# The skip term of a chunked scan as diagonal matrix products on TensorE, with one GpSimd sum left

## What is computed

```
y_fwd = ssd_chunked(xs, dt[:, :, 0], a_neg[0], bm, cm)
y_bwd = flip(ssd_chunked(flip(xs), flip(dt[:, :, 1]), a_neg[1], flip(bm), flip(cm)))
y = y_fwd + y_bwd + d_skip.astype(jnp.float32).reshape(SSD_GROUPS, hg)[..., None] * xs
y = y.reshape(b, s, SSD_INNER) * jax.nn.silu(z.astype(jnp.float32))
```

## Time and profile before

| | us |
|---|---|
| runs | 2482.91, 2483.04, 2487.15; median 2483.04 |
| profiled execution, its own time | 2485.22 |
| span of its trace | 2483.4 |
| PE busy in the span | 2426.9 (98%) |
| chain that ended last: PE 81%, DVE 9%, ACT 4%, POOL 3%, issue 2%, DMA 1% | |
| chunk loop, layer 0, start of L1081 of chunk 0 to low part of chunk 0 after the loop | 404.56 to 477.11 |
| the same, layer 1 | 1631.25 to 1704.39 |

### The profile page before, as it was taken

One profiled execution on the slowest core, in us unless ns is written; L12 is line 12 of the kernel. 1 busy time (PEld: TensorE's weight loads), 2 busy tenths in 40 slices (PEclk: granted clock), 3 DMA queues, 4 the chain that ended last, 5 costly groups with the idle time before them and its releaser, 6 DMA issues.

```text
span 2483.4 us, 33046 instructions
## 1 busy us (share of the span) xinstructions
PE 2426.9 (98%) x12882; PEld 2072.2 (83%) x12882; DVE 1375.8 (55%) x1561; ACT 998.4 (40%) x1737; POOL 1263.1 (51%) x814
## 2 busy tenths in 40 slices
PE   7999999999999999999999999998999999999999
PEld 6989997887888888887898899977878888888887
DVE  4476557738655546428345765586385555544332
ACT  4345567613444344212024465585144344431110
POOL 3242113323977877666633311142349877866664
PEclk9999999999999999999999999999999999999999
DMA  4434444231222212654333334442212222226544
GB/s 160 136 114 125 134 139 149 81 119 68 85 79 91 85 68 85 217 178 132 130 121 94 110 128 151 134 136 90 89 64 102 85 70 100 83 90 201 174 141 142
DMA packets 102964, 290.68 MB, mean 117 GB/s; under 512 B 7800, under 2 KB 30328, under 8 KB 101112
## 3 DMA queue, kind: packets, MB, share of 16 engines
q1 hardware_dynamic: 80360, 255.73, 30.4%
q10 hardware_dynamic: 22456, 32.90, 4.1%
HBM read 229.84 MB, written 58.75 MB: 116 GB/s over the span
## 4 chain that ended last, share of the span: by engine, by line
PE 81%; DVE 9%; ACT 4%; POOL 3%; issue 2%; DMA 1%; SPq 0%; ACTq 0%; DVEq 0%; POOLq 0%
PE PS L690 20%; PE PS L694 20%; PE PS L693 20%; PE PS L775 3%; PE PS L779 3%; PE PS L778 3%; PE PS L945 2%; PE PS L934 2%; POOL WL L629 2%; DVE HL L1780 1%; PE PS L1116 1%; PE PS L1081 1%; PE PS L924 1%; PE PS L923 1%; ACT LG L1501 1%
## 5 line engine op out<-in xcount | busy, mean ns | idle before, releaser
L605 POOL CAST WH<-RAW 128x1024 fp32r<-128x1024 f32 x156 | 184.5, 1182 | 905.5 <-PE PS L690 327.1
L690 PE MATMUL PS<-HH,WH 128*128 128x512 f32 x1264 | 496.4, 393 | 3.6 <-ACT QS L1668 2.6
L694 PE MATMUL PS<-HH,WL 128*128 128x512 f32 x1264 | 493.3, 390 | 0.0
L693 PE MATMUL PS<-HL,WH 128*128 128x512 f32 x1104 | 430.5, 390 | 0.0
L607 POOL TENSOR_TENSOR WL<-RAW,WH 128x1024 fp32r<-128x1024 f32 x156 | 396.8, 2543 | 12.5
L690 PEld LDWEIGHTS PS<-HH,WH 128*128 128x128 f32 x1264 | 237.4, 188 | 56.5 <-DVE HL L1780 3.5
L694 PEld LDWEIGHTS PS<-HH,WL 128*128 128x128 f32 x1264 | 237.3, 188 | 51.9
L690 PE MATMUL PS<-AR,WH 128*128 128x512 f32 x704 | 276.0, 392 | 2.3 <-DVE X L2208 1.8
L694 PE MATMUL PS<-AR,WL 128*128 128x512 f32 x704 | 275.9, 392 | 0.0
L693 PE MATMUL PS<-AR,WH 128*128 128x512 f32 x704 | 275.2, 391 | 0.0
L775 PE MATMUL PS<-WH,HH 128*128 128x256 f32 (+1 forms) x896 | 261.0, 291 | 1.7 <-ACT KN L1307 1.3
(11 more groups left out here) (274 smaller groups left out, 4677.3 us busy)
## 6 DMA issues: line engine op xcount, KB each, us to landing
RAW<-wst SPq DMA_DIRECT2D x156, 512.0 KB, 3.5
TOE<-toe_d SPq DMA_DIRECT2D x64, 512.0 KB, 3.7
act_d<-CVV SPq DMA_DIRECT2D x22, 1024.0 KB, 4.0
ARL<-act_d SPq DMA_DIRECT2D x88, 256.0 KB, 3.3
RAW<-wst SPq DMA_DIRECT2D x20, 1024.0 KB, 4.9
RAWB<-wst SPq DMA_DIRECT2D x20, 1024.0 KB, 4.9
XBS<-xbc_d SPq DMA_DIRECT2D x24, 512.0 KB, 4.2
xbc_d<-CV ACTq DMA_DIRECT2D x16, 512.0 KB, 3.6
```

Source lines behind the costliest of these rows:

```text
L605: nc.gpsimd.tensor_copy(hi, raw).then_inc(hi_done, 1)
L690: ins = nc.tensor.matmul(out, wh, xh, start=first, stop=False, skip_group_check=onto)
L693: nc.tensor.matmul(out, wh, xl, start=False, stop=False, skip_group_check=onto)
L694: return nc.tensor.matmul(out, wl, xh, start=False, stop=last, skip_group_check=onto)
```

## The change

The skip term leaves GpSimd. A diagonal matrix `DIAG` (four 128x128 tiles, one for two heads each: identity times d_skip) is made once in each layer by one VectorE instruction at the head of `far()`. In each chunk TensorE multiplies the four x tiles of `XBS`, as they came by DMA, with it, straight into bank 4, ahead of the turn of the next chunk; the value product then accumulates onto it instead of starting the bank. The wait for `chunk_done` of the chunk before (bank 4 read) moves from the value product to these products, and `xbs_used` is given by the last of them. GpSimd keeps one sum, `Y3` = `Y1` + `Y2`, in chunks 1 to 6; in chunk 0 VectorE adds `Y2` and in chunk 7 `Y1` to the bank by itself.

```diff
@@ -266,6 +266,7 @@
         ZG = place("ZG", [P, 2, 3, UC], u_at + 8192)
+        DIAG = place("DIAG", [P, 4, P], u_at + 29952)
...
@@ -653,17 +653,11 @@
-                    pool.wait_ge(chunk_done, 1 + n)
-                    step.then(nc.gpsimd.tensor_tensor(by_head(Y3[:]), xs, per_head(par_("d_skip")), ALU.mult))
-                    if c < LINKS:
+                    if 0 < c < LINKS:
+                        pool.wait_ge(chunk_done, 1 + n)
+                        pool.wait_ge(y12_done, 1 + l * LINKS + c)
                         pool.wait_ge(y2_ready, l * LINKS + c + 1)
-                        ins = nc.gpsimd.tensor_tensor(Y3[:], Y3[:], Y2[:], ALU.add)
-                        if c:
-                            step.then(ins)
-                    if c:
-                        pool.wait_ge(y12_done, 1 + l * LINKS + c)
-                        ins = nc.gpsimd.tensor_tensor(Y3[:], Y3[:], Y1[:], ALU.add)
-                    ins.then_inc(y3_ready, 1)
+                        nc.gpsimd.tensor_tensor(Y3[:], Y1[:], Y2[:], ALU.add).then_inc(y3_ready, 1)
...
@@ -1091,8 +1085,11 @@
                                      start=False, stop=True, skip_group_check=True).then_inc(mx_full, 1)
-                    pe.wait_ge(yo_full, n + 1)
-                    pe.sem_inc(xbs_used, 1)
+                    pe.wait_ge(chunk_done, 1 + n)
+                    for j in range(4):
+                        last = nc.tensor.matmul(PS[:, 4, j * P:(j + 1) * P], XBS[:, par, j, :], DIAG[:, j], start=(j == 0),
+                                                stop=False, skip_group_check=True)
+                    last.then_inc(xbs_used, 1)
...
@@ -1108,13 +1105,13 @@
                     pe.wait_ge(xs_ready, n + 1)
-                    pe.wait_ge(chunk_done, 1 + n)
...
-                                                    XS[:, par, e * HD:(e + 1) * HD], start=True, stop=True)
+                                                    XS[:, par, e * HD:(e + 1) * HD], start=False, stop=True,
+                                                    skip_group_check=True)
...
@@ -2074,6 +2071,9 @@
                 def far():
+                    TT(DIAG[:].rearrange("p j (a e) -> p j a e", a=2),
+                       ident.rearrange("p (a e) -> p a e", a=2).unsqueeze(1).to_broadcast((P, 4, 2, HD)),
+                       par_("d_skip").rearrange("p (j a) -> p j a", a=2).unsqueeze(3).to_broadcast((P, 4, 2, HD)), ALU.mult)
...
@@ -2169,8 +2169,11 @@
                         dve.wait_ge(yd_full, 2 + n + 1)
-                        dve.wait_ge(y3_ready, n + 1)
-                        TT(Y1[:], Y3[:], bank(4), ALU.add).then_inc(chunk_done, 1)
+                        if c == 0:
+                            dve.wait_ge(y2_ready, k + 1)
+                        elif c < LINKS:
+                            dve.wait_ge(y3_ready, l * (LINKS - 1) + c)
+                        TT(Y1[:], (Y3 if 0 < c < LINKS else Y1 if c else Y2)[:], bank(4), ALU.add).then_inc(chunk_done, 1)
```

More of the change, by code:

```diff
@@ L348, in trunk @@
         far_ready, ldt_ready = sem("far_ready"), sem("ldt_ready")
-        y3_ready, p_step = sem("y3_ready"), sem("p_step")
+        y3_ready = sem("y3_ready")
         exp_ready, w_masked, yo_full, sf_full = sem("exp_ready"), sem("w_masked"), sem("yo_full"), sem("sf_full")
@@ L591, in _ @@
             pool.sem_inc(w_ready, 2)
-            step = Steps(pool, p_step)
             def split(u, s, skipped):
```

## The result

| | median us | lowest to highest | runs |
|---|---|---|---|
| before | 2486.78 | 2482.91 to 2488.64 | 20 |
| changed | 2491.78 | 2486.26 to 2498.14 | 20 |

The ratio is 1.0021, with a 95% interval of 1.0013 to 1.0029: the changed kernel is 5.2 us slower, 3.2 to 7.2. The forecast was a difference of +4.7 us and a time of 2487.8 us, range 2484.5 to 2491.5. The difference came; the time lies 0.3 us above the range, because the 2483.04 us on which it was built was the middle of three runs, and 17 more moved that median to 2486.78.

A forecast was written before the change was run, and what follows sets the result against it. TensorE, busy 98% of the span, bounds the kernel. Layer 0 (0.69 + 0.00 + 2.73 - 0.85 = +2.57) and layer 1 (0.69 + 0.09 + 3.59 - 2.20 = +2.17) give +4.7: 2487.8 us, range 2484.5 to 2491.5.

The forecast's parts named there:

- The products: Four diagonal products per chunk take 0.90 us, on TensorE's path in chunks 0 to 6; chunks 1 to 6 take 9.25 each.
- The rival of cheap products: In each chunk, four products cost only 0.44 us, like transposes; 2481.4, or 2485.8 with waits back; chance 0.06.
- The collision: In the chunks, VectorE's L2144 and GpSimd's sum exclude each other; race stays open, but the new products hide any loss.
- a cover of 0.09 us: If GpSimd's sum wins, L2144 releases the value product's second half at T + 8.30; TensorE arrives at T + 8.39.
- an L2144 of 1.65 in some chunks without cost: Sign of being right: VectorE's L2144 still shows 1.65 us in some chunks, hidden by the new products.
- the loss of chunk 2: By the port rule alone, chunk 2's collision loss would stay, since GpSimd's remaining sum starts on the same signal.
- The rival of a collision that comes through: In the chunks, Y2 finishes later and the sum goes first; at 0.4 later 3.7 us, 2491.5; chance 0.09.
- `DIAG` and chunk 0: Ahead of chunk 1: making DIAG costs 0.69 us per layer; chunk 0 adds 0.00 in layer 0, +0.09 in layer 1.
- The ends: At the loop's end, removed GpSimd sums give back 0.85 us in layer 0 and 2.20 in layer 1.
- The clock: After the loop, TensorE's clock falls in further stretches, 1.7 us loss, 2489.5, chance 0.19; or recovers, 2486.1, chance 0.09.
- a difference outside the two loops: Sign of being wrong: the time difference lies outside the chunk loops of the two layers; no size given.
- its differences are then put onto the median, 2483.04: Whole kernel: +4.7 us, derived from the profiled execution of 2485.22, is added to the median, giving 2487.8.

The follow-up runs named there:

- e2: Kernel before with DIAG and the four products added, their result overwritten, GpSimd keeping all three steps: 2494.11 us, ratio 1.0031 to before.
- e1: Changed kernel without the diagonal products and without DIAG, skip term missing from the output: 2478.74 us, ratio 0.9966 to before.
- e5: Changed kernel with 19 small unused identity products in TensorE's gaps after the loop: 2489.59 us, ratio 1.0009 to before.
- e4: Kernel before with only GpSimd's two additions exchanged, Y1 ahead of Y2: 2480.15 us, ratio 0.9974 to before.
- e3: Changed kernel with DIAG made by GpSimd in place of VectorE, and TensorE waiting for it: 2491.77 us, ratio 1.0018 to before.
- e6: Kernel before with 19 small unused identity products in TensorE's gaps after the loop: 2486.35 us, ratio 0.9997 to before.

## Why the prediction was right, and where it was wrong

**The products.** Right: 0.89 for four against 0.90, and all of it on the path: 9.24 us in each of chunks 1 to 6, forecast 9.25. Chunks 1 to 6 cost +2.67 and +3.51, forecast +2.73 and +3.59. The rival of cheap products is refuted by the same row, and by e2.

**The collision.** That it costs nothing was right, the reason only half. The forecast left the race open and counted on a cover of 0.09 us; in the trace VectorE won it in every chunk and the cover was never used. Its own sign, an L2144 of 1.65 in some chunks without cost, did not come. e1 and e2 say why: with one sum left VectorE's chunk begins on TensorE's signal and L2144 goes first even without the products; and with the products it goes first even with three steps on GpSimd. Either half of the change is enough, and the forecast had derived neither. The rule of the Trainium skill (SBUF — State Buffer, section "Who interferes with whom") holds for the one that comes second (1.76 in place of 1.28 for GpSimd's sum), and the time that the prediction drew from it, the loss of chunk 2 kept, did not come, because the sum did not come first. The rival of a collision that comes through is refuted.

**`DIAG` and chunk 0.** Forecast +0.69 and +0.78, trace +1.45 and +0.70. `DIAG` itself took 0.64. Layer 0's excess is clock: granted 0.72 at 404 to 408 us in this execution, and in e5, whose trace has 1.00 there, the same stretch is +0.58.

**The ends.** Forecast -0.85 and -2.20, trace -0.93 and -2.46; layer 1 came near its bound of 2.40 and passed it by 0.06.

**The clock.** The rival was seen and under-sized. It was priced as one stretch of 1.7 us in one layer, with a chance of 0.19. The profiled execution shows the projection late in both layers (0.88 + 2.89 and 0.87 - 0.06 = 4.6 us), with more elsewhere. The forecast had named a difference outside the two loops as a sign of being wrong; in this pair of traces +7.86 of 12.8 lie outside the rows of the change. The late stretch needs no products. In e1, which has none of them, layer 0's projection starts at half clock as well, 479.13 - 478.70 = 0.43 us from start to start:

```profile
478.70 0.63 PE L719 MATMUL PS<-HH,WL 128*128 128x512 f32 x1
479.13 0.63 PE L718 MATMUL PS<-HH,WH 128*128 128x512 f32 x1
```

There layer 0's first tile takes 9.27 us, and in e4 9.15, against 10.10 in the changed kernel and 7.21 before; in e2 and e3, which have the products, it takes 7.25 and 7.26. In layer 1 it takes 8.77 to 9.93 in all of these, before among them. Each is one execution.

Over the changed kernel's 20 executions it is a matter of degree: those at a mean granted clock of 0.998 took 2486.26 to 2489.93 us, those at 0.996 2491.67 to 2493.63, those at 0.993 to 0.995 2494.25 to 2498.14. Before's 20 span 5.7 us, the changed kernel's 11.9. Its lowest run is 3.4 us above before's lowest, its median 5.0: some 1.7 us of the median's difference go with the wider spread, and e5, which fills the gap, brings back 2 to 3, if anything. At full clock the trace gives the loops +4.94 - 0.87 = +4.1, and e5's trace, whose loops are at full clock throughout, gives the same +4.1 in these rows. That the rest of the median's +5.0 is clock is likely but not shown. At a mean clock of 0.999 there are one execution of e6 (2482.05 us) and two of e5 (2486.96 and 2488.15), 4.9 to 6.1 apart at nearly one clock: more than +4.1, and too few to settle it. That loops and clock add up to the forecast +4.7 is partly luck: the forecast had no clock in its sum, and its own terms came out some 0.7 us high.

**The step that failed** is "its differences are then put onto the median, 2483.04", with the range drawn from that base. The three runs already lay 4.2 us apart (2482.91 to 2487.15), two of them at the low end, and the profiled one was at 2485.22. The median of 20 is 2486.78: 3.74 us more, nearly as much as the whole change. With that base the same sum gives 2491.5 against 2491.78. The range of 2484.5 to 2491.5 took in the bounds of the terms and none of the scatter of the base: 4 us of seen spread should have widened it at the top by some 2 us.

What stays open: why the clock falls at 1140 to 1148 us in one execution and not in another, or longer at 48 to 60, where nothing was changed; why it falls late after the loop in some of these kernels; and how much of the median's +5.0 it holds. No run here separates that.

## What to carry to other kernels

Work that is moved from an engine off the path to the one that is full costs its whole length each time, and may hide the very wait it was meant to remove: measure the relief alone and the cost alone before joining them, since here the relief alone brought about 8 us, and the products cost about 8 without it (e2) and about 13 with it. Where two engines exclude each other at a late signal, first look whether one instruction of the pair can be put earlier in its own queue by order alone; exchanging two additions brought 6.5 us and added nothing. The smaller the forecast difference, the more runs its base needs: three runs whose spread is as large as the change can carry the difference but not the time.

## What the runs showed of the hardware

- The stretch at 1.2 GHz after the loop keeps to no place in the program. In the profiled execution of the changed kernel it came some twelve microseconds later than before (granted 0.53 and 0.50 from 484 to 492 us, before 0.50 at 472 to 476), out of a stretch where TensorE had time into one where it had none. Ahead of it TensorE had been busy for 1.10 of the 4.00 us from 480 to 484; in e5, with products in those gaps, the clock stayed at 1.00.
- What filling the gaps was worth depended on the clock when the filling began. In e5 it was up (1.00), and the projection came 0.87 us earlier in each layer. In before it was down, the first of the same products ran at half clock (2.93 us for ten, 2.28 at full), the next turn was delayed, and nothing was gained.
- Half clock nearly doubles a projection product's time, 0.43 against 0.23 us from start to start, and on the path that made 2.9 us in one tile of layer 0. In chunk 7 of before the same half clock shows hardly any price: 11.12 us to the first low part in layer 0, against 11.00 in e2, where the clock was full until then.
- A race between VectorE and GpSimd that is decided by 0.03 to 0.08 us was still decided the same way every time: for VectorE in chunks 1 to 6 of both layers in the changed kernel, e1, e2, e3, e4 and e5, one profiled execution of each.
